# Attention of a hybrid decoder step: high and low parts of Q, K and V stacked in the array, two passes in place of three

## The reference, cut to what matters

```python
def one_block(args):                       # one block of 128 queries
    s = jnp.einsum("bqhd,bkhd->bhqk", q_blk, k, preferred_element_type=jnp.float32) * scale
    s = s + fq_blk[..., :, None] - fk_t[:, :, None, :]
    s = jnp.where(kpos[None, :] <= pos_blk[:, None], s, -jnp.inf)
    pr = jax.nn.softmax(s, axis=-1)
    return jnp.einsum("bhqk,bkhd->bqhd", pr.astype(v.dtype), v)
```

## Time and profile before

| | |
|---|---|
| median of three runs | 2957.08 us |
| profiled execution | 2950.17 us |
| its span | 2948.3 us, 43435 instructions |
| PE busy | 2835.5 us (96%) |
| DVE busy | 1349.3 us (46%) |
| ACT busy | 833.0 us (28%) |
| mean granted clock of PE | 0.975 of full |
| attention, from 1266 to 1975 us | 709 us; PE busy 679.72, DVE 362.57, ACT 274.42 |

### The profile page before, as it was taken

How to read it: one execution, slowest core, us unless ns; L and a number is a source line. 1 busy time by engine, 2 the same in 40 slices (tenths; PEclk the granted TensorE clock), 3 DMA queues, 4 the chain that set the end, 5 groups by cost and what they waited for, 6 DMA issues and landing times.

```text
span 2948.3 us, 43435 instructions
## 1 busy us (share of the span) xinstructions
PE 2835.5 (96%) x18210; PEld 2746.0 (93%) x18210; DVE 1349.3 (46%) x1795; ACT 833.0 (28%) x1314; POOL 158.0 (5%) x92
## 2 busy tenths in 40 slices
PE   7898999999999999999999999989999999999996
PEld 6898999999999999988888888879999999999995
DVE  6666354244244344444555544554542442442443
ACT  5556321111111122333334333342211110211222
POOL 1010200000000000210000000001000000000003
PEclk9999999999999999999999999989999999999998
DMA  3112211111111111222211222101111111111111
GB/s 122 36 36 66 76 43 39 53 48 38 51 50 41 48 50 39 59 82 66 73 52 58 73 80 66 51 30 44 43 40 56 45 43 52 43 43 53 43 41 70
DMA packets 86669, 158.10 MB, mean 54 GB/s; under 512 B 17490, under 2 KB 51506, under 8 KB 86354
## 3 DMA queue, kind: packets, MB, share of 16 engines
q1 hardware_dynamic: 86482, 155.33, 16.8%
HBM read 141.60 MB, written 13.70 MB: 53 GB/s over the span
## 4 chain that ended last, share of the span: by engine, by line
PE 92%; ACT 3%; DVE 2%; issue 2%; DMA 0%; POOL 0%; DVEq 0%; SPq 0%; ACTq 0%; POOLq 0%
PE psum L330 78%; PE psum L1023 4%; PE psum L1075 3%; PE psum L1047 2%; PE psum L1062 1%; PE psum L1008 1%; PE psum L1026 1%; DVE PTL L1430 0%; DVE SB L1405 0%; PE psum L877 0%; DVE X L1457 0%; ACT L678 0%; DVE VS L433 0%; ACT TM L692 0%; ACT L690 0%
## 5 line engine op out<-in xcount | busy, mean ns | idle before, releaser
L330 PE MATMUL psum<-XH,WH 128*128 128x352 f32 x2904 | 642.6, 329 | 1.7 <-issue 1.7
L330 PE MATMUL psum<-XH,WL 128*128 128x352 f32 x2904 | 628.8, 324 | 0.0
L330 PE MATMUL psum<-XL,WH 128*128 128x352 f32 x2904 | 628.5, 325 | 0.0
L312 ACT ACTIVATE WH<-WR 128x1024 fp32r<-128x1024 f32 (+2 forms) x217 | 215.3, 993 | 1041.0 <-PE psum L330 1029.8
L330 PEld LDWEIGHTS psum<-XH,WL 128*128 128x128 f32 x2904 | 499.2, 188 | 1.6
L330 PEld LDWEIGHTS psum<-XL,WH 128*128 128x128 f32 x2904 | 494.7, 188 | 1.6
L330 PEld LDWEIGHTS psum<-XH,WH 128*128 128x128 f32 x2904 | 490.0, 190 | 4.0 <-issue 2.3
L1315 DVE TENSOR_TENSOR X<-psum,X 128x1056 f32<-128x1056 f32 x64 | 80.5, 1258 | 383.3 <-PE psum L330 383.3
L321 DVE TENSOR_TENSOR WL<-WR,WH 128x1024 fp32r<-128x1024 f32 (+2 forms) x217 | 246.2, 1134 | 10.3 <-ACT WH L312 9.9
L330 PE MATMUL psum<-FYH,WH 128*128 128x352 f32 x1152 | 249.2, 324 | 0.0
L330 PE MATMUL psum<-FYH,WL 128*128 128x352 f32 x1152 | 248.3, 323 | 0.0
(11 more groups left out here) (206 smaller groups left out, 3435.8 us busy)
## 6 DMA issues: line engine op xcount, KB each, us to landing
WR<-in_wfi SPq DMA_DIRECT2D x96, 512.0 KB, 3.5
WR<-in_wfo SPq DMA_DIRECT2D x64, 384.0 KB, 3.0
WR<-in_wa SPq DMA_DIRECT2D x24, 512.0 KB, 3.6
WR<-in_wqkv SPq DMA_DIRECT2D x24, 512.0 KB, 4.5
X<-in_xT SPq DMA_DIRECT2D x16, 528.0 KB, 5.4
CC<-in_ck SPq DMA_DIRECT2D x128, 64.0 KB, 1.8
NF<-nf_scratch SPq DMA_DIRECT2D x16, 512.0 KB, 4.4
CC<-in_cv SPq DMA_DIRECT2D x128, 64.0 KB, 1.9
```

The costliest lines, as they stand in the source:

```text
L312: nc.scalar.activation(WH[:, par, 0:n], WR[:, par, 0:n], ACT.Copy).then_inc(w_hi, 1)
L330: mm = nc.tensor.matmul(psum[0:m, 3 * slot + c, 0:CH], w, x[:, k, c * CH:(c + 1) * CH], start=(k == 0 and part == 0), stop=(k == nk - 1 an ...
```

## The change

The high and low parts of one operand now lie in the same matmul.

- **Logits.** QHL of a head has its high part on one half of the partitions and its low part on the other. KHH has K's high part on both halves, KLL its low part on both. Two matmuls, QHL with KHH and QHL with KLL, on 128 partitions take the place of three on 64. ACT and DVE write one half of KHH and KLL each, and SP copies it to the other half by DMA (four more DMAs per pair). The four ACT copies and four DVE subtractions, each 64 partitions x 1024, stand in slot 17 of the pair before (`heads_hi`, `heads_lo`); before they were two and two of 128 partitions at the head of the pair.
- **Values.** VV has the high and the low part of a head's V side by side, 128 columns. Two matmuls per key block, with the high and with the low probabilities, take the place of three; the output has 128 partitions, one half from V's high part, the other from its low part. ACT copies one half to X (counted by `o_half`), and DVE adds the other half to it (`o_read`), a new instruction in slots 3 to 18.
- **Pair head.** PE runs unit 0 ahead of `values`, and the two projection steps follow.
- **Room.** PTH and PTL become separate tiles; VS shares its place with PTH1, so the first write of PTH1 in a pair waits for V's output DMA (`v_out`).

```diff
+                wait(sp, s_read, u0)
+                sp.dma_start(NF[:, :], ins["nf"][2 * hp, :].partition_broadcast(P)).then_inc(nf_ld, 16)
+                kll = [KLL[0], KLL1_last if last else KLL[1]]
+                sp.wait_ge(k_hi, 2 * (c + 1) + 4 * t)
+                for h in range(2):
+                    sp.dma_start(KHH[h][HALF[1 - h], :].bitcast(F32), KHH[h][HALF[h], :].bitcast(F32)).then_inc(kh_dup, 16)
+                sp.wait_ge(k_lo, 2 * (c + 1) + 4 * t)
+                for h in range(2):
+                    sp.dma_start(kll[h][HALF[1 - h], :].bitcast(F32), kll[h][HALF[h], :].bitcast(F32)).then_inc(kl_dup, 16)
                 sp.wait_ge(acc_read, J_QKV + 3 * c + 3 + 6 * t)
                 sp.dma_start(outs["v"][hp], VS[:, :]).then_inc(v_out, 16)
...
+            def heads_hi(c, t):
+
+                wait(act, qk_done, UNITS * c + 2 * UNITS * t)
                 act.wait_ge(acc_read, J_QKV + 3 * c + 2 + 6 * t)
-                nc.scalar.activation(QH[:, :], QS[:, 0:SEQ], ACT.Copy).then_inc(q_hi, 1)
-                nc.scalar.activation(KH[:, :], KS[:, 0:SEQ], ACT.Copy).then_inc(k_hi, 1)
-                wait(act, pv_done, u0)
+                wait(act, kh_dup, 32 * c + 64 * t)
+                for h, rows in enumerate(HALF):
+                    nc.scalar.activation(KHH[h][rows, :], KS[rows, 0:SEQ], ACT.Copy).then_inc(k_hi, 1)
+                for h, rows in enumerate(HALF):
+                    nc.scalar.activation(QHL[h][rows, :], QS[rows, 0:SEQ], ACT.Copy).then_inc(q_hi, 1)
...
-                        nc.scalar.activation(PTH[:, (v - 1) % 2, 0:n], T_ps[:, 0:n],
+                        if v == 2:
+                            act.wait_ge(v_out, 16 * (c + 1) + 32 * t)
+                        nc.scalar.activation(PTH[(v - 1) % 2][:, 0:n], T_ps[:, 0:n],
...
-                            nc.scalar.activation(X[HD * h:HD * (h + 1), hp, P * i:P * (i + 1)],
-                                                 O_ps[0:HD, 0:P], ACT.Copy).then_inc(o_read, 1)
+                            nc.scalar.activation(X[HALF[h], hp, P * i:P * (i + 1)],
+                                                 o_unit(v - 2)[HALF[1 - h], :], ACT.Copy).then_inc(o_half, 1)
...
                     h, i = UNIT_OF[v]
-                    rows, q, n = slice(HD * h, HD * (h + 1)), slice(P * i, P * (i + 1)), P * (i + 1)
+                    q, n = slice(P * i, P * (i + 1)), P * (i + 1)
+                    kll = KLL1_last if last and h == 1 else KLL[h]
                     for a in range(0, n, 512):
                         b = min(a + 512, n)
-                        for x, y, part in ((QH, KH, 0), (QH, KL, 1), (QL, KH, 2)):
-                            nc.tensor.matmul(S_ps[:, a:b], x[rows, q], y[rows, a:b], start=(part == 0),
+                        for y, part in ((KHH[h], 0), (kll, 1)):
+                            nc.tensor.matmul(S_ps[:, a:b], QHL[h][:, q], y[:, a:b], start=(part == 0),
                                              stop=False, skip_group_check=True)
...
-                    pe.wait_ge(o_read, u0 + v)
-                    cols = slice(HD * h, HD * (h + 1))
+                    if v <= 2:
+                        pe.wait_ge(o_half, u0 + 1)
+                    if v > 2:
+                        pe.wait_ge(o_read, 2 * NQB * c + v - 2 + 4 * NQB * t)
                     for kb in range(i + 1):
                         keys = slice(P * kb, P * (kb + 1))
-                        for x, y, part in ((VH, PTH, 0), (VH, PTL, 1), (VL, PTH, 2)):
-                            mm = nc.tensor.matmul(O_ps[0:HD, 0:P], x[:, kb, cols], y[:, v % 2, keys],
-                                                  start=(kb == 0 and part == 0), stop=(kb == i and part == 2))
+                        vhl = VV[:, kb, 2 * h:2 * h + 2, :].rearrange("p a d -> p (a d)")
+                        for y, part in ((PTH[v % 2], 0), (PTL[v % 2], 1)):
+                            mm = nc.tensor.matmul(o_unit(v), vhl, y[:, keys],
+                                                  start=(kb == 0 and part == 0), stop=(kb == i and part == 1),
+                                                  skip_group_check=True)
                     mm.then_inc(pv_done, 1)
 
-                values()
...
                     if v < UNITS:
                         logits(v)
-                    if v > 0:
-                        for _ in range(KSTEPS[v]):
-                            project()
+                    if v == 0:
+                        values()
+                    for _ in range(KSTEPS[v]):
+                        project()
...
+                for v in range(UNITS + 2):
                     if v < UNITS:
...
+                    if v >= 3:
+
+                        h, i = UNIT_OF[v - 2]
+                        dve.wait_ge(o_half, u0 + v - 1)
+                        x = X[HALF[h], hp, P * i:P * (i + 1)]
+                        nc.vector.tensor_tensor(x, o_unit(v - 2)[HALF[h], :], x, ALU.add).then_inc(o_read, 1)
+                    if v == UNITS and c < NHP - 1:
+                        heads_lo(c + 1, t)
                     if v - 1 in SPLIT_SLOTS and c < NHP - 1:
...
-                    if v >= 2:
+                    if v == 0:
+                        values_lo(c, t)
+                    if 2 <= v <= UNITS:
                         m = P * (UNIT_OF[v - 1][1] + 1)
                         dve.wait_ge(pt_hi, u0 + v)
                         dve.wait_ge(pv_done, u0 + max(v - 2, 1))
```

More of the change, by code:

```diff
@@ L98, in sem @@
             return ctx.enter_context(nc.semaphore(name))
+        o_x7 = end[0] + 4 * (KT - 1) * T
         X = at("X", [P, KT, T], F32, region(KT * T))
@@ L798, in jq @@
                     return J_QKV + 3 * c + r, 6, t
[L800 to L809 removed]
+                if c == 0:
+                    heads_hi(0, 0)
                 for v in range(UNITS + 2):
+                    if v == UNITS and c < NHP - 1:
+                        heads_hi(c + 1, t)
                     if v < UNITS:
@@ L989, in values @@
                     wait(pe, pt_lo, (UNITS - 1) * (c + 2 * t))
-                    wait(pe, o_read, u0)
+                    wait(pe, o_half, u0)
+                    wait(pe, o_read, 2 * NQB * (c + 2 * t))
                     for kb in range(NQB):
@@ L1375, in _, with heads_lo, q_low, k_low @@
             dve.wait_ge(f_out, 32 * FSTEPS)
+            def heads_lo(c, t):
+                wait(dve, kl_dup, 32 * c + 64 * t)
+                wait(dve, qk_done, UNITS * c + 2 * UNITS * t)
+                kll = [KLL[0], KLL1_last if c == NHP - 1 else KLL[1]]
+                def q_low(h):
+                    dve.wait_ge(q_hi, 2 * c + 1 + h + 4 * t)
+                    nc.vector.tensor_tensor(QHL[h][HALF[1 - h], :], QS[HALF[h], 0:SEQ],
+                                            QHL[h][HALF[h], :].bitcast(F32), ALU.subtract).then_inc(q_lo, 1)
+                def k_low(h):
+                    dve.wait_ge(k_hi, 2 * c + 1 + h + 4 * t)
+                    if c == NHP - 1 and h == 1:
+                        dve.wait_ge(q_lo, 2 * NHP)
+                        dve.wait_ge(qd_done, 4 * NHP)
+                    nc.vector.tensor_tensor(kll[h][HALF[h], :], KS[HALF[h], 0:SEQ],
+                                            KHH[h][HALF[h], :].bitcast(F32), ALU.subtract).then_inc(k_lo, 1)
+                for h in range(2):
+                    q = QS[HALF[h], SEQ:T].rearrange("p (b j) -> p b j", j=DS)
+                    nc.vector.tensor_copy(QXd[HALF[h], :, DS * h:DS * (h + 1)], q).then_inc(qd_done, 1)
+                    nc.vector.tensor_copy(QD[HALF[h], :, h, :], q).then_inc(qd_done, 1)
+                if c < NHP - 1:
+                    k_low(0)
+                    k_low(1)
+                    q_low(0)
+                    q_low(1)
+                else:
+                    k_low(0)
+                    q_low(0)
+                    q_low(1)
+                    k_low(1)
@@ L1377, in pair, with values_lo @@
+            def values_lo(c, t):
+                dve.wait_ge(v_hi, c + 1 + 2 * t)
+                nc.vector.tensor_tensor(VV[:, :, 0:4:3, :], T_ps[:, 0:SEQ].rearrange("p (a h d) -> p a h d", h=2, d=HD),
+                                        VV[:, :, 1:3, :].bitcast(F32), ALU.subtract).then_inc(v_lo, 1)
             def pair(c, t):
                 hp, u0 = c + 2 * t, UNITS * c + 2 * UNITS * t
-                if c > 0:
+                if c == 0:
+                    heads_lo(0, 0)
+                else:
@@ L1380, in pair @@
                     v_in(c, t)
-                dve.wait_ge(q_hi, c + 1 + 2 * t)
-                nc.vector.tensor_tensor(QL[:, :], QS[:, 0:SEQ], QH[:, :].bitcast(F32), ALU.subtract
-                                        ).then_inc(q_lo, 1)
-                for h in range(2):
-                    rows = slice(HD * h, HD * (h + 1))
-                    q = QS[rows, SEQ:T].rearrange("p (b j) -> p b j", j=DS)
-                    nc.vector.tensor_copy(QXd[rows, :, DS * h:DS * (h + 1)], q).then_inc(qd_done, 1)
```

(3 more changed lines are left out.)

70 lines of the change are left out of this document (39 added, 31 removed).

## The result

The changed kernel takes 3075.49 us (median of four runs, 3071.72 to 3076.83) against 2954.99 for the kernel before on the same chip: ratio 1.0403, 95% interval 1.0383 to 1.0424. The forecast was 2994 us in a range of 2945 to 3030. The direction was right, the size was not: the loss on the profiled execution is 3.4 times the one worked out (127 us for 37).

What follows compares the result with a forecast made beforehand. The VectorE-ScalarE ring was to replace TensorE as the bound in attention: +4.4 us per pair in pairs 0 to 6 (31 us) and +6 in pair 7, together +37, giving 2994 us, range 2945 to 3030.

Steps and rivals of the forecast that it cites:

- The product without gain: Products on TensorE: 0.107 us per 128-column matmul, 0.214 per key block instead of 0.18; with seams gone, 3.4 us less.
- the logits' seams: Logits on TensorE: switches into and out of the 64-partition form, 0.11 and 0.10 us, vanish 128 times, saving 26.9 us.
- The ring through the copy and the addition: Slots 3 to 16: VectorE's addition waits for ScalarE's last copy, lengthening their mutual waiting by 11.2 us in 14 slots.
- The displaced instructions: Loop pair, slots 3 to 16: four VectorE weight splits and scalings now stand behind the addition, costing 4.6 us.
- Rivals B and C: B: TensorE stays bound, addition hidden, 2900 us, chance 0.12. C: displaced instructions hidden, 2962 us, no change, chance 0.12.
- The ring's slots: Slots 3 to 16 of a loop pair: 61.6 us against 56.0, so 5.6 us longer.
- the ring's hops: Slots 5 and 6, read in pair 7: later starts lengthen the two slots by 1.53 us, from 6.02 to 7.55.
- The pair's end: From the end of slot 16 into the next pair's head: 1.2 us less per loop pair.
- The stall ahead of the last product: Pair's end: TensorE is ready for unit 16's product at 6.3 us, its low part at 9.7: 3.4 us stall.
- TensorE's savings: TensorE has 65 us less to do, 8.1 per pair; some shorten the pair's end, for instance 1.4 us at slot 17.
- Pair 7: Last pair's slots: ring 55.4 us plus NF's wait 0.8 and low clock 1.3, against 47.9: 9.6 us longer.
- Rival D: As the main forecast, but the 3.4 us stall also lowers the clock, 3.5 us in seven pairs: 3019 us, chance 0.14.

Runs made afterwards that it cites:

- e1_wait_only: Kernel before, with only a wait of VectorE for ScalarE's copy put behind the reduction, nothing added: 2993.9 us, ratio 1.0121.
- e2_add_last: Changed kernel with VectorE's addition moved to the end of its slot, behind the low part of the unit before: 2915.5 us, ratio 0.9857 to the kernel before.
- e6_moved_ahead: Changed kernel with the low weight parts and the scaling of Q and K ahead of VectorE's addition: 3045.4 us, ratio 1.0303 to the kernel before.
- e7_swap_halves: Changed kernel with the product's halves exchanged: ScalarE copies the half it writes to, VectorE adds the other: 3073.9 us, ratio 1.0399 to the kernel before.
- e10_heads_behind: Changed kernel with the next pair's splits behind unit 16's high and low parts in slot 17, addition left in place: 3040.0 us, ratio 1.0280 to before.
- e5_values_only: Kernel before with only the values' half of the change, including copy and addition; logits and splits as before: 3097.2 us, ratio 1.0494.
- e8_fill: Changed kernel with small unread matmuls filling TensorE's idle time ahead of the transposes, more in pair 7: 3101.4 us, ratio 1.0493 to the kernel before.
- e4_logits_only: The change's logits half alone; values and product as in the kernel before, no addition on VectorE: 2894.5 us, ratio 0.9789 to the kernel before.

## Why the prediction fell short

**What held.** The change of bound: TensorE was full, and is no longer. The product without gain (0.107 forecast, 0.11 measured), and of the logits' seams all but 0.05 us each. The ring through the copy and the addition, shown by e1_wait_only and e2_add_last. The displaced instructions: forecast 4.6 us per pair, and e6_moved_ahead takes away 5.6 with the projection's waits. Rivals B and C are out: TensorE idles, and nothing hides the displaced work.

**The ring's slots, +5.6 forecast, +12.0 measured** (the 14 slots of the forecast, 56.4 to 68.3). The mechanism was right; the term that failed by size is the ring's hops, put at 1.53 us for two slots. I read them in one slot of head 0 in pair 7, where all instructions started at partition 0, outside the loop, and took 0.03 us for the hand-over from ScalarE to VectorE from a read-out. The changed kernel has longer intervals: 0.12 and 0.14 us on ScalarE in head 0; 0.12 there and about 0.23 on VectorE in head 1, from the reciprocal and the low part (1656.86 to 1657.25 against 1619.27 to 1619.54, with the same 256 columns); and, in the loop's four pairs alone, 0.12 at the hand-over. Over eight slots of head 0 and six of head 1 that is 5.9 us in a loop pair and 4.2 in a written-out one, 5.1 in the mean of pairs 0 to 6, beside a surplus of 6.4 (7.7 in the loop's pairs, 4.6 in the others). The projection's waits have a part in it too: e6_moved_ahead takes away 1.0 more than the 4.6 forecast. Not every slot pays in full, as where TensorE is late. For ScalarE e7_swap_halves shows the cause; the sum is a count of rows, and no run took all of these intervals away.

**The pair's end, -1.2 forecast, +2.3 measured** (from the end of slot 16; 33.8 to 36.1). Failed, with its sign. The stall ahead of the last product, forecast at 3.4 us, is 4.2 in the mean (29.3 us in seven pairs); and I let TensorE's savings pay for it. e10_heads_behind gives back 4.8 us per pair, more than the whole excess, and e2_add_last, where TensorE sets the pace, has neither stall nor loss (34.1 from reduction 16 on, against 37.3 before). So the savings count where TensorE is the bound and not behind the ring; that this is the whole of it is argued, not shown. e5_values_only, with no moved splits, still has 40.1, and why stays open.

**Pair 7, +9.6 in the slots forecast, +21.5 measured** (47.9 to 69.4). Failed: to 4.2 us of longer intervals comes the clock, priced at 1.3 and worth 5.1 there by e8_fill. Together that is 8.0 of the 11.9 that are missing; 4 us stay open. Rival D had the mechanism, but put it in the other seven pairs, where its size is open.

In sum: 7 x 6.4 + 7 x 3.5 + 11.9 = 81 of the 90 us between the forecast for the profiled execution (2987) and the measured one (3077).

## What to carry to other kernels

When a change adds a wait between two engines that already wait for each other, draw the new ring and price each hand-over from the row that most resembles it in engine, kind and first partition, for each head or half apart, and inside a hardware loop apart from outside; savings of the old bound do not count once the ring is longer. Put the consumer of a neighbour's last instruction at the end of its slot, or one unit later, and anything that nobody awaits ahead of the wait. Here the half that costs no new wait (e4_logits_only, 2894.5 us, ratio 0.9789) beats both kernels.

## What the runs showed of the hardware

- In these traces ScalarE starts an instruction 0.12 to 0.14 us later when the group of partitions in which its operand starts differs from the last one used in the same memory: 0.21 in place of 0.09 from the read-out to the high part, 0.41 in place of 0.27 from the high part to the copy. VectorE does the same by 0.11 to 0.12 us (0.32 in place of 0.21, 0.39 in place of 0.27).
- From the end of ScalarE's copy to VectorE's addition that waits for it: 0.03 us in the written-out pairs, 0.14 in the pairs of the hardware loop (64 additions each). From a read-out's end to the reciprocal: 0.03 in both (kernel before).
- Two product passes with 128 stationary columns take longer than three with 64: 2 x 0.11 against 3 x 0.06 us per key block.
- A pair in which TensorE waits in every slot fell to a mean granted clock of 0.59; filled with small matmuls it had 0.91.
